# Two PSUM banks per vector and scalar instruction in the feed-forward parts of a hybrid decoder layer (fp32, one core)

## The chip, the cores and the metric

The kernel runs on one core of one Trainium2 chip. The metric is the device time of one execution in microseconds; given are three executions of the kernel before, and one more was recorded by the hardware profiler. Engines are called PE (matrix products), DVE (vector), ACT (scalar), POOL and SP. POOL only builds constants here and SP only starts transfers.

## What is computed

One step of a hybrid decoder layer on 1024 prompt tokens and 8 x 4 sample tokens, 1056 in all, width 1024, in fp32. The parts that the change touches are the two feed-forward parts:

```
def rmsnorm(x, g):
    y = x * rsqrt(mean(x * x) + EPS)
    return y * g

def swiglu_ffn(x, w_gu, w_down):
    gate, up = split(x @ w_gu)          # D_FF = 2816 each
    return (silu(gate) * up) @ w_down

x = x + 0.5 * rmsnorm(swiglu_ffn(rmsnorm(x, g1), w_gu1, w_down1), g2)
x = x + mixer(x)                        # convolution and RG-LRU heads, one projection in, one out
x = x + 0.5 * rmsnorm(swiglu_ffn(rmsnorm(x, g3), w_gu2, w_down2), g4)
x = x + rmsnorm(sigmoid(rmsnorm(x, g5) @ w_gate) * (p @ w_proj), g6)
```

## The kernel before, in words

**Layout.** Features lie on the 128 partitions, tokens along the free axis. The 1056 tokens are three chunks of C = 352 (c = 0, 1, 2). Every fp32 product is three matmuls of a high and a low part (`passes`, lines 589 to 591): x_hi, x_lo, the weights' w_hi, w_lo and wd_hi, wd_lo, and the hidden values' a_hi, a_lo. ACT makes a high part by a copy, DVE the low part by a subtraction. The first norm's gain is folded into the weights, its 1/rms (`rstd_pre`) is multiplied onto the products.

**Steps.** D_FF is worked in NI = 11 steps of G = 2 blocks of 128. A step has, per chunk, four gate and up products of 24 matmuls (into four PSUM banks: g0, g1, u0, u1), and later eight down products of 6 matmuls (m = 0 to 7) that DVE adds into `acc`. In steps 2 to 10 (a hardware loop, `ffn_step`) the order on PE is the gate and up products of chunks 0, 1, 2 and then the down products of chunks 0, 1, 2. In the last step (`ffn_last`) each chunk's down products stand right behind its gate and up products, so that the norm behind the part can begin chunk by chunk. The first step of part 1 follows the tokens as they come in; the first step of part 2 (`ffn_first`) has the down products of chunks 0 and 1 behind chunk 1 and those of chunk 2 behind chunk 2.

**Banks.** Six PSUM banks are a ring, `ps`. `ring_plan` numbers each use n of the whole program, use n lies in bank n mod 6, and PE may write it when `psum_free` has reached n - 5; the reader counts `psum_free` up by one for each bank. Two more banks (`ps_aux`) hold the small products of the norms.

**From products to hidden values.** On DVE `scaled` reads g0, g1, u0, u1 one by one (line 1583); ACT takes the silu of each half (`silu`, line 1089); DVE multiplies each half (`hidden`, line 1594); ACT rounds each half to a_hi (`hidden_hi`, line 1098); DVE makes each half of a_lo (`hidden_lo`, line 1600), upon which PE's `down_products` may begin. `down` (lines 1645 and 1650) reads the down products' banks one by one.

**Order.** It is written out by hand for each engine; each runs its own list in order and waits on counters. In the last step DVE's list for chunk 1 and 2 puts between the eight `down` the four parts of `apply_pair` for the chunk before (lines 1554 to 1568: 1/rms, gain, residual, low part, squares into `ssum`, line 1526); PE waits for the finished sum of squares with its small product of line 628.

```
                    hidden_chunk(f, i, c, tiles(f, i), hook)
                    pair(0)
                    for m in range(KT):
                        down(f, i, c, m)
                        if m in (2, 5, 7):
                            q = 1 + (2, 5, 7).index(m)
                            pair(q)
```

At the start, PE turns the parameter rows and the state rows into one bank (lines 752 to 756), and DVE copies it out in three pieces (lines 1718 to 1720).

Of the kernel before, what the change touches and what calls it, by code (L numbers as in the profile page):

```python
# [62 lines left out]
def ring_plan():  # L63
# [9 lines left out]
    for c in range(NC):  # L73
        for k in range(KT):
            put("xT", c, k)
        if c == 0:
            put("params")
        n += 4
# [109 lines left out]
def cols(c):  # L188
    return slice(C * c, C * c + C)


def build(nc, a, out):
    ctx = ExitStack()
    with ctx:
# [250 lines left out]
        def _(sp_eng):  # L445
# [94 lines left out]
            eng.wait_ge(a_lo_done, 2 * NI * NC * G)  # L540
# [36 lines left out]
        def _(eng):  # L577
# [67 lines left out]
            def down_products(f, i, c):  # L645
                Q, off = NI * NC * G * f, down_at(f, i, c)
                eng.wait_ge(a_lo_done, i * (NC * G) + (Q + 2 * c + 2))
# [97 lines left out]
            for c in range(NC):  # L745
# [3 lines left out]
                if c == 0:  # L749
# [3 lines left out]
                    eng.transpose(dst[:, P:P + CW * NJ], rows[0:CW * NJ, P:2 * P],  # L753
                                  ident[0:CW * NJ, 0:CW * NJ])
# [242 lines left out]
        def _(eng):  # L997
# [84 lines left out]
            def silu(f, i, c, h):  # L1082

                R, Q = RING["ffn", f], NI * NC * G * f
                q, n = NC * G * i + (Q + 2 * c + h), STEP * i + (gate_at(f, i, c) + h)
                eng.wait_ge(psum_free, n + 1)
                if f or not isinstance(i, int) or i or c:
                    eng.wait_ge(prod_done, q - 1)
                eng.activation(tmp_s[:, h, :], tmp_g[:, h, :], ACT.Silu).then_inc(silu_done, 1)  # L1089

            def hidden_hi(f, i, c, h):

                R, Q = RING["ffn", f], NI * NC * G * f
                eng.wait_ge(prod_done, NC * G * i + (Q + 2 * c + h + 1))
# [3 lines left out]
                eng.activation(a_hi[:, h, cols(c)], tmp_a[:, h, :], ACT.Copy).then_inc(a_hi_done, 1)  # L1098

            def hidden_chunk(f, i, c, next_half, hook=None):  # L1100
# [3 lines left out]
                silu(f, i, c, 0)  # L1104
                hook("g0")
                silu(f, i, c, 1)
# [5 lines left out]
                hidden_hi(f, i, c, 0)  # L1112
                hidden_hi(f, i, c, 1)
# [352 lines left out]
        def _(eng):  # L1466
# [16 lines left out]
            def bank_at(reg, n):  # L1483

                eng.wait_ge(psum_full, reg + (n + 1))
                return ps[:, n % BANKS, 0:C]
# [88 lines left out]
            def scaled(f, i, c, h, up):  # L1575

                R, Q = RING["ffn", f], NI * NC * G * f
                q, off = NC * G * i + (Q + 2 * c + h), gate_at(f, i, c) + 2 * up + h
                src = bank_at(i * STEP, off)
                if f or not isinstance(i, int) or i or c:  # L1580

                    eng.wait_ge(prod_done if up else silu_done, q - 1)
                eng.tensor_tensor((tmp_u if up else tmp_g)[:, h, :], src, rstd_pre[:, cols(c)],  # L1583
                                  ALU.mult).then_inc(psum_free, 1)

            def hidden(f, i, c, h):

                R, Q = RING["ffn", f], NI * NC * G * f
                q, n = NC * G * i + (Q + 2 * c + h), STEP * i + (gate_at(f, i, c) + 2 + h)
                eng.wait_ge(silu_done, q + 1)  # L1590
                eng.wait_ge(psum_free, n + 1)
                if f or not isinstance(i, int) or i or c:
                    eng.wait_ge(a_lo_done, q - 1)
                eng.tensor_tensor(tmp_a[:, h, :], tmp_s[:, h, :], tmp_u[:, h, :], ALU.mult  # L1594
                                  ).then_inc(prod_done, 1)

            def hidden_lo(f, i, c, h):
                q = NC * G * i + (NI * NC * G * f + 2 * c + h)
                eng.wait_ge(a_hi_done, q + 1)
                eng.tensor_tensor(a_lo[:, h, cols(c)], tmp_a[:, h, :], f32(a_hi[:, h, cols(c)]),  # L1600
                                  ALU.subtract).then_inc(a_lo_done, 1)

            def hidden_chunk(f, i, c, next_tile, hook=None):
# [5 lines left out]
                scaled(f, i, c, 0, 0)  # L1609
                hook("g0")  # L1610
                scaled(f, i, c, 1, 0)
# [630 lines left out]
```

## Time and profile before

| | |
|---|---|
| device time, three executions | 2345.4, 2345.52, 2349.55 us; median 2345.52 us |
| profiled execution, first to last instruction (span) | 2337.7 us |
| its own device time | not listed apart; the median stands 7.8 us above the span |
| PE busy | 2158.0 us, 92% of the span, 13020 matmuls |
| DVE busy | 1317.6 us, 56%, 2620 instructions |
| ACT busy | 769.8 us, 33%, 1500 instructions |
| mean granted PE clock | 0.959 of full speed |
| moved by DMA | 116.15 MB, mean 50 GB/s |

Busy time overlaps between engines. A busy share tells how full an engine is, not what sets the end; for that one reads who waited for whom, and in which stretch. The loops of the two feed-forward parts lie at about 125 to 745 us and 1427 to 2047 us; the last steps reach to about 860 us and 2160 us.

### The profile page before, as it was taken

To read this page: it belongs to the slowest core of one execution; us is meant where nothing else is said; L and a number is where in the kernel's file an instruction comes from. 1 tells how busy PE (TensorE), PEld (TensorE's weight loads), DVE (VectorE), ACT (ScalarE), POOL (GpSimd) and SP (SyncE) were. 2 spreads that over 40 slices of the span, in tenths; PEclk is the share of its full clock that TensorE was granted. 3 is DMA by queue.
4 is the path that set the end of the run, shared out by engine and by line. 5 is a ranking of instruction groups with operands and counts; after the bars stand their busy time and mean duration, and the time that the engine had idled before them with its cause. 6 is when DMAs were issued, how large, how long until landed. Compare 5 with 4: busy or idle time off the path is not lost. (4 is left out here: it accounts for less than half of the span.)

```text
span 2337.7 us, 34611 instructions
## 1 busy us (share of the span) xinstructions
PE 2158.0 (92%) x13020; PEld 2106.1 (90%) x13020; DVE 1317.6 (56%) x2620; ACT 769.8 (33%) x1500; POOL 0.9 (0%) x8
## 2 busy tenths in 40 slices
PE   5899999999999878999989689999999999995886
PEld 5899999999999878887789689999999999995886
DVE  4544444543445666988555764545434554557686
ACT  4311121221122333365575532212221121225563
POOL 0000000000000000000000000000000000000000
PEclk8999999999999889999999889999999999998897
DMA  4101111101111011100014201111101111102222
GB/s 149 37 28 45 54 54 54 54 27 35 45 54 54 1 45 41 46 1 19 19 38 144 91 1 55 55 54 54 45 18 45 54 54 54 54 1 73 72 91 75
DMA packets 92360, 116.15 MB, mean 50 GB/s; under 512 B 4596, under 2 KB 83704, under 8 KB 92282
## 3 DMA queue, kind: packets, MB, share of 16 engines
q1 hardware_dynamic: 91065, 110.79, 14.4%
q10 hardware_dynamic: 1216, 4.33, 0.6%
q8 instruction: 48, 0.79, 0.1%
q14 instruction: 31, 0.25, 0.0%
HBM read 110.15 MB, written 4.95 MB: 49 GB/s over the span
## 5 line engine op out<-in xcount | busy, mean ns | idle before, releaser
L589 PE MATMUL ps<-x_hi,w_lo 128*128 128x352 f32 x2688 | 883.2, 329 | 17.8 <-DVE w_lo L1503 8.8
L590 PE MATMUL ps<-x_lo,w_hi 128*128 128x352 f32 x2688 | 872.9, 325 | 0.0
L591 PE MATMUL ps<-x_hi,w_hi 128*128 128x352 f32 x2688 | 871.9, 324 | 0.0
L589 PEld LDWEIGHTS ps<-x_hi,w_lo 128*128 128x128 f32 x2688 | 514.6, 191 | 19.1 <-DVE w_lo L1503 9.5
L590 PEld LDWEIGHTS ps<-x_lo,w_hi 128*128 128x128 f32 x2688 | 515.3, 192 | 0.0
L591 PEld LDWEIGHTS ps<-x_hi,w_hi 128*128 128x128 f32 x2688 | 513.5, 191 | 0.0
L589 PE MATMUL ps<-a_hi,wd_lo 128*128 128x352 f32 x1104 | 361.6, 328 | 24.6 <-DVE a_lo L1600 11.6
L590 PE MATMUL ps<-a_lo,wd_hi 128*128 128x352 f32 x1104 | 357.7, 324 | 0.0
L591 PE MATMUL ps<-a_hi,wd_hi 128*128 128x352 f32 x1104 | 357.3, 324 | 0.0
L1650 DVE TENSOR_TENSOR acc<-ps,acc 128x352 f32<-128x352 f32 x480 | 249.3, 523 | 88.7 <-PE ps L591 82.8
L1583 DVE TENSOR_TENSOR tmp_u<-ps,rstd_pre 128x352 f32<-128x352 f32 x132 | 69.1, 524 | 370.7 <-PE ps L591 370.7
L1022 ACT ACTIVATE w_hi<-raw,params 128x256 fp32r<-128x256 f32 x512 | 213.6, 496 | 132.0 <-DMA raw<-in_ffn_w_gu_dram 109.1
L1503 DVE SCALAR_TENSOR_TENSOR w_lo<-raw,params,w_hi 128x256 fp32r<-128x256 f32 x512 | 225.8, 477 | 46.7 <-ACT w_hi L1022 46.7
L1089 ACT ACTIVATE tmp_s<-tmp_g 128x352 f32<-128x352 f32 x132 | 65.3, 498 | 552.1 <-DVE tmp_g L1583 552.1
L589 PEld LDWEIGHTS ps<-a_hi,wd_lo 128*128 128x128 f32 x1104 | 210.4, 191 | 27.6 <-DVE a_lo L1600 12.8
L590 PEld LDWEIGHTS ps<-a_lo,wd_hi 128*128 128x128 f32 x1104 | 210.9, 191 | 0.0
L591 PEld LDWEIGHTS ps<-a_hi,wd_hi 128*128 128x128 f32 x1104 | 210.1, 190 | 0.0
L1583 DVE TENSOR_TENSOR tmp_g<-ps,rstd_pre 128x352 f32<-128x352 f32 x132 | 68.5, 522 | 244.1 <-PE ps L591 230.0
L1098 ACT ACTIVATE a_hi<-tmp_a 128x352 fp32r<-128x352 f32 x132 | 59.9, 494 | 418.4 <-DVE tmp_a L1594 418.4
L829 PE MATMUL ps<-gp,diag 128*128 128x352 f32 (+1 forms) x360 | 108.8, 460 | 3.5 <-ACT diag L1284 3.5
L1526 DVE TENSOR_TENSOR ssum<-ssum,sq 128x352 f32<-128x352 f32 x177 | 92.6, 523 | 22.3 <-ACT sq L1048 9.5
L829 PEld LDWEIGHTS ps<-gp,diag 128*128 128x128 f32 x360 | 69.2, 194 | 38.1 <-issue 5.5
(172 smaller groups left out, 1678.2 us busy)
## 6 DMA issues: line engine op xcount, KB each, us to landing
raw<-in_ffn_w_gu_dram SPq DMA_DIRECT2D x88, 512.0 KB, 3.5
rawd<-in_ffn_w_down_dram SPq DMA_DIRECT2D x22, 1024.0 KB, 7.6
raw<-in_w_out_dram SPq DMA_DIRECT2D x24, 512.0 KB, 3.5
raw<-in_ple_w_gate_dram SPq DMA_DIRECT2D x24, 512.0 KB, 3.4
raw<-in_w_in_dram SPq DMA_DIRECT2D x16, 512.0 KB, 4.0
x_in<-in_x_prompt_dram ACTq DMA_DIRECT2D x6, 512.0 KB, 7.8
out_dram<-y_stage SPq DMA_DIRECT2D x6, 512.0 KB, 2.8
rawd<-in_ple_w_proj_dram SPq DMA_DIRECT2D x1, 1024.0 KB, 7.2
```

The lines of the kernel that those rows point to most:

```text
L589: eng.matmul(dst, wl, xh, start=first, stop=False)
L590: eng.matmul(dst, wh, xl, start=False, stop=False)
L591: return eng.matmul(dst, wh, xh, start=False, stop=last)
L829: mm = eng.matmul(dst[:, 0:w], diag[:, tap, :], gp[:, j, at0:at0 + w], start=tap == 0, stop=tap == TP - 1)
L1022: ins = eng.activation(w_hi[s][:, sl], raw[:, sl], ACT.Copy, scale=vec(gain, k))
L1089: eng.activation(tmp_s[:, h, :], tmp_g[:, h, :], ACT.Silu).then_inc(silu_done, 1)
L1098: eng.activation(a_hi[:, h, cols(c)], tmp_a[:, h, :], ACT.Copy).then_inc(a_hi_done, 1)
L1503: ins = eng.scalar_tensor_tensor(w_lo[s][:, sl], raw[:, sl], vec(gain, k), f32(w_hi[s][:, sl]), ALU.mult, ALU.subtract)
L1526: eng.tensor_tensor(ssum[:, i % 2, :], ssum[:, i % 2, :], sq[:, (ADD0[i] + m - 1) % SQ, :], ALU.add).then_inc(add_done, 1)
L1583: eng.tensor_tensor((tmp_u if up else tmp_g)[:, h, :], src, rstd_pre[:, cols(c)], ALU.mult).then_inc(psum_free, 1)
L1650: eng.tensor_tensor(acc[:, m, cols(c)], src, acc[:, m, cols(c)], ALU.add).then_inc(psum_free, 1)
```

## The change

DVE and ACT take the two banks of a pair in one instruction of 2 x 352 elements: `scaled` reads g0 and g1 together, then u0 and u1 together; `silu`, `hidden`, `hidden_hi` and `hidden_lo` work on both halves at once; `down` reads banks m and m + 1. A reader waits until both banks are full, and counts `psum_free` up by two. Since the pairs have to begin on an even bank, the states at the start get a ring use of their own ("states"). Where `ffn_last` put `apply_pair` behind m = 2, 5, 7 it now stands behind the pairs that begin at m = 2, 4, 6.

```
@@ ring_plan
         if c == 0:
             put("params")
+            put("states")
@@ PE, start
+                    mm.then_inc(psum_full, 1)
+                    dst = bank(RING["states"], 512)
                     for j in range(NJ):
-                        mm = eng.transpose(dst[:, 2 * P + 32 * j:2 * P + 32 * j + 32],
+                        mm = eng.transpose(dst[:, 32 * j:32 * j + 32],
                                            st_rows[0:32, j * P:j * P + P], ident[0:32, 0:32])
@@ ACT
-            def silu(f, i, c, h):
+            def silu(f, i, c):
...
-                eng.activation(tmp_s[:, h, :], tmp_g[:, h, :], ACT.Silu).then_inc(silu_done, 1)
+                eng.activation(tmp_s[:, :, :], tmp_g[:, :, :], ACT.Silu).then_inc(silu_done, 1)
...
-                eng.activation(a_hi[:, h, cols(c)], tmp_a[:, h, :], ACT.Copy).then_inc(a_hi_done, 1)
+                eng.activation(a_hi[:, :, cols(c)], tmp_a[:, :, :], ACT.Copy).then_inc(a_hi_done, 1)
@@ DVE
-            def bank_at(reg, n):
+            def banks_at(reg, n):
+                assert n % 2 == 0 and BANKS % 2 == 0
+                eng.wait_ge(psum_full, reg + (n + 2))
+                return ps[:, n % BANKS:n % BANKS + 2, 0:C]
...
+            def scaled(f, i, c, up):
+                q, off = NC * i + (NI * NC * f + c), gate_at(f, i, c) + G * up
+                src = banks_at(i * STEP, off)
                 if f or not isinstance(i, int) or i or c:
+                    eng.wait_ge(prod_done if up else silu_done, q)
+                eng.tensor_tensor((tmp_u if up else tmp_g)[:, :, :], src,
+                                  rstd_pre[:, cols(c)].unsqueeze(1).broadcast_to([P, G, C]),
+                                  ALU.mult).then_inc(psum_free, G)
+            def hidden(f, i, c):
+                q, n = NC * i + (NI * NC * f + c), STEP * i + (gate_at(f, i, c) + G)
                 eng.wait_ge(silu_done, q + 1)
-                eng.wait_ge(psum_free, n + 1)
+                eng.wait_ge(psum_free, n + G)
...
+                eng.tensor_tensor(a_lo[:, :, cols(c)], tmp_a[:, :, :], f32(a_hi[:, :, cols(c)]),
                                   ALU.subtract).then_inc(a_lo_done, 1)
...
-                src = bank_at(i * STEP, off)
+                src = banks_at(i * STEP, off)
+                dst = acc[:, m:m + 2, cols(c)]
                 if isinstance(i, int) and i == 0:
-                    eng.tensor_copy(acc[:, m, cols(c)], src).then_inc(psum_free, 1)
+                    eng.tensor_copy(dst, src).then_inc(psum_free, 2)
                     return
...
+                eng.tensor_tensor(dst, src, dst, ALU.add).then_inc(psum_free, 2)
@@ DVE, ffn_last
-                    for m in range(KT):
+                    for m in range(0, KT, 2):
                         down(f, i, c, m)
-                        if m in (2, 5, 7):
-                            q = 1 + (2, 5, 7).index(m)
+                        if m:
+                            q = m // 2
                             pair(q)
@@ DVE, start
-                eng.tensor_copy(params[:, width:3 * P], src[:, width:3 * P]).then_inc(psum_free, 1)
+                eng.tensor_copy(params[:, P:P + CW * NJ], src[:, P:P + CW * NJ]).then_inc(psum_free, 1)
+                eng.wait_ge(psum_full, RING["states"] + 1)
+                eng.tensor_copy(params[:, width:3 * P], ps[:, RING["states"] % BANKS, 0:P]
+                                ).then_inc(psum_free, 1)
```

PE's list keeps its products and their order; only what it waits for counts differently. Two places on the other engines show what moved.

DVE, the last step of feed-forward part 1, chunk 1, before: from the read of u0 and u1 (tmp_u) over the hidden values to the first `down` (acc<-ps,acc) and the next part of the norm's application. In brackets are the counters waited for: prod_done the hidden product, silu_done the silu, a_hi_done the high part, psum_full PE, dve_own and psum_free among others DVE's own.

```order
L1583 TENSOR_TENSOR tmp_u<-ps,rstd_pre 128x352 [waits prod_done,psum_full] x2
L1594 TENSOR_TENSOR tmp_a<-tmp_s,tmp_u 128x352 [waits a_lo_done,psum_free,silu_done] x2
L1600 TENSOR_TENSOR a_lo<-tmp_a,a_hi 128x352 [waits a_hi_done] x2
L1554 TENSOR_TENSOR acc<-acc,rstd_post 128x2x352 [waits aux_free]
L1559 SCALAR_TENSOR_TENSOR acc<-acc,half_g,x_hi 128x352 [waits dve_own]
L1559 SCALAR_TENSOR_TENSOR acc<-acc,half_g,x_hi 128x352
L1563 TENSOR_TENSOR acc<-acc,x_lo 128x2x352 [waits dve_own]
L1650 TENSOR_TENSOR acc<-ps,acc 128x352 [waits psum_free,psum_full] x3
L1554 TENSOR_TENSOR acc<-acc,rstd_post 128x2x352 [waits aux_free]
```

And now:

```order
L1583 TENSOR_TENSOR tmp_u<-ps,rstd_pre 128x704 [waits prod_done,psum_full]
L1594 TENSOR_TENSOR tmp_a<-tmp_s,tmp_u 128x704 [waits a_lo_done,psum_free,silu_done]
L1599 TENSOR_TENSOR a_lo<-tmp_a,a_hi 128x2x352 [waits a_hi_done]
L1555 TENSOR_TENSOR acc<-acc,rstd_post 128x2x352 [waits aux_free]
L1560 SCALAR_TENSOR_TENSOR acc<-acc,half_g,x_hi 128x352 [waits dve_own]
L1560 SCALAR_TENSOR_TENSOR acc<-acc,half_g,x_hi 128x352
L1564 TENSOR_TENSOR acc<-acc,x_lo 128x2x352 [waits dve_own]
L1646 TENSOR_TENSOR acc<-ps,acc 128x2x352 [waits psum_free,psum_full] x2
L1555 TENSOR_TENSOR acc<-acc,rstd_post 128x2x352 [waits aux_free]
```

Three pairs of instructions became three single ones, each of which waits for the whole of the one before it; and ahead of the second L1555 stand four banks of down products instead of three.

ACT, the first step of part 1, chunk 2, before: the table and silu of each half, the high part of the down weights (wd_hi, two blocks of 1024), and the high parts of the next step's weights and of the hidden values.

```order
L1089 ACT_TABLE_LOAD [waits prod_done]
L1089 ACTIVATE tmp_s<-tmp_g 128x352 [waits psum_free]
L1033 ACTIVATE wd_hi<-rawd 128x2048 [waits rawd_in]
L1089 ACTIVATE tmp_s<-tmp_g 128x352 [waits prod_done,psum_free]
L1022 ACTIVATE w_hi_51<-raw,params 128x256 [waits raw_in0,psum_full]
L1022 ACTIVATE w_hi_51<-raw,params 128x256 x3
L1098 ACTIVATE a_hi<-tmp_a 128x352 [waits prod_done] x2
```

And now:

```order
L1091 ACT_TABLE_LOAD [waits prod_done]
L1091 ACTIVATE tmp_s<-tmp_g 128x704 [waits psum_free]
L1036 ACTIVATE wd_hi<-rawd 128x2048 [waits rawd_in]
L1025 ACTIVATE w_hi_51<-raw,params 128x256 [waits raw_in0,psum_full]
L1025 ACTIVATE w_hi_51<-raw,params 128x256 x3
L1100 ACTIVATE a_hi<-tmp_a 128x2x352 [waits prod_done]
```

The down weights' high part now stands behind the silu of both halves instead of one.

## Rows read from the trace of the kernel before

**Rows 1.** The page's first part: busy time, share of the span, instructions of each engine.
```profile
PE 2158.0 (92%) x13020; PEld 2106.1 (90%) x13020; DVE 1317.6 (56%) x2620; ACT 769.8 (33%) x1500; POOL 0.9 (0%) x8
```
**Rows 2.** Busy us (x instructions) of PE, PEld, DVE, ACT, POOL; clock; DMA; one loop stretch.
```profile
200.00:269.00 69.00, 69.00 (x436) 69.00 (x435) 32.34 (x65) 14.01 (x29) 0.00 (x0) 1.00 0.14 46
```
**Rows 3.** Who waited for whom, PE: total us, times, longest us; whole span.
```profile
PE ps_aux L628 <- DVE ssum L1526: 71.9, 10, 11.8
PE ps L589 <- DVE a_lo L1600: 11.6, 5, 2.6
...
PE ps L589 <- issue: 6.7, 3, 2.6
...
PE ps L739 <- DVE x_lo L1757: 5.3, 4, 3.0
...
PE ps L589 <- DVE acc L1645: 0.5, 1, 0.5
```
**Rows 4.** Groups by line and shape: busy us, mean ns of one, idle us before.
```profile
L1650 DVE TENSOR_TENSOR acc<-ps,acc 128x352 f32<-128x352 f32 x480 | 249.3, 523 | 88.7 <-PE ps L591 82.8
...
L1098 ACT ACTIVATE a_hi<-tmp_a 128x352 fp32r<-128x352 f32 x132 | 59.9, 494 | 418.4 <-DVE tmp_a L1594 418.4
...
L1563 DVE TENSOR_TENSOR acc<-acc,x_lo 128x704 f32<-128x704 f32 x44 | 39.2, 892 | 1.5
...
L1077 ACT ACTIVATE x_hi<-acc 128x704 fp32r<-128x704 f32 x32 | 25.4, 793 | 115.6 <-DVE acc L1563 115.6
```
**Rows 5.** DVE in order of time, last step of part 1, chunk 1: start, us, instruction, [idle before].
```profile
787.15 0.52 DVE L1583 TENSOR_TENSOR tmp_u<-ps,rstd_pre 128x352 f32<-128x352 f32 x1 [4.02 <-PE ps L591]
787.59 0.95 DVE L1594 TENSOR_TENSOR tmp_a<-tmp_s,tmp_u 128x352 f32<-128x352 f32 x2
788.67 0.96 DVE L1600 TENSOR_TENSOR a_lo<-tmp_a,a_hi 128x352 fp32r<-128x352 f32 x2
789.54 0.89 DVE L1554 TENSOR_TENSOR acc<-acc,rstd_post 128x704 f32<-128x704 f32 x1
...
792.39 1.38 DVE L1650 TENSOR_TENSOR acc<-ps,acc 128x352 f32<-128x352 f32 x3
793.68 0.88 DVE L1554 TENSOR_TENSOR acc<-acc,rstd_post 128x704 f32<-128x704 f32 x1
794.60 1.08 DVE L1559 SCALAR_TENSOR_TENSOR acc<-acc,half_g,x_hi 128x352 f32<-128x352 f32 x2
```
**Rows 6.** PE in order of time, the same step: chunk 1's down products, and the norm's sum.
```profile
789.68 0.43 PE L589 MATMUL ps<-a_hi,wd_lo 128*128 128x352 f32 x1 [2.57 <-DVE a_lo L1600]
...
811.34 1.44 PE L628 MATMUL ps_aux<-ones,ssum 128*128 128x1 f32 x6 [6.12 <-DVE ssum L1526]
```
**Rows 7.** PE after two such waits: busy us (x matmuls), granted clock, DMA.
```profile
761.00:764.00 3.00, 3.00 (x10) 0.50 0.02 5
...
2062.40:2065.40 3.00, 3.00 (x19) 1.00 0.02 5
```
**Rows 8.** Chunk 0 of part 2's last step: PE's first down matmul, DVE's fourth `down`.
```profile
2062.34 0.40 PE L589 MATMUL ps<-a_hi,wd_lo 128*128 128x352 f32 x1 [2.62 <-issue]
...
2066.43 0.53 DVE L1650 TENSOR_TENSOR acc<-ps,acc 128x352 f32<-128x352 f32 x1 [0.43 <-PE ps L591]
```
**Rows 9.** Last step of part 1, chunk 2: u1, ACT's high parts of weights, DVE's low parts.
```profile
824.73 0.52 DVE L1583 TENSOR_TENSOR tmp_u<-ps,rstd_pre 128x352 f32<-128x352 f32 x1 [3.46 <-PE ps L591]
...
826.56 0.89 ACT L1022 ACTIVATE w_hi<-raw,params 128x256 fp32r<-128x256 f32 x2
...
828.28 0.88 DVE L1503 SCALAR_TENSOR_TENSOR w_lo<-raw,params,w_hi 128x256 fp32r<-128x256 f32 x2 [1.07 <-ACT w_hi L1022]
```
**Rows 10.** ACT between chunk 0 and chunk 1 of the start.
```profile
48.46 0.45 ACT L1190 ACTIVATE x_hi<-ps 128x352 fp32r<-128x352 f32 x1
```
**Rows 11.** DVE at the start: the copies of parameters and states.
```profile
20.27 0.27 DVE L1718 COPY params<-ps 128x104 f32<-128x104 f32 x1 [1.21 <-PE ps L756]
...
20.64 0.28 DVE L1720 COPY params<-ps 128x128 f32<-128x128 f32 x1
```

More of the change, by code:

```diff
@@ L645, in down_products @@
             def down_products(f, i, c):
-                Q, off = NI * NC * G * f, down_at(f, i, c)
-                eng.wait_ge(a_lo_done, i * (NC * G) + (Q + 2 * c + 2))
+                Q, off = NI * NC * f, down_at(f, i, c)
+                eng.wait_ge(a_lo_done, i * NC + (Q + c + 1))
                 for m in range(KT):
@@ L1590, in hidden, with hidden_lo @@
                 eng.wait_ge(silu_done, q + 1)
-                eng.wait_ge(psum_free, n + 1)
+                eng.wait_ge(psum_free, n + G)
                 if f or not isinstance(i, int) or i or c:
-                    eng.wait_ge(a_lo_done, q - 1)
-                eng.tensor_tensor(tmp_a[:, h, :], tmp_s[:, h, :], tmp_u[:, h, :], ALU.mult
+                    eng.wait_ge(a_lo_done, q)
+                eng.tensor_tensor(tmp_a[:, :, :], tmp_s[:, :, :], tmp_u[:, :, :], ALU.mult
                                   ).then_inc(prod_done, 1)
[L1597 to L1600, printed above, removed]
+            def hidden_lo(f, i, c):
+                eng.wait_ge(a_hi_done, NC * i + (NI * NC * f + c + 1))
+                eng.tensor_tensor(a_lo[:, :, cols(c)], tmp_a[:, :, :], f32(a_hi[:, :, cols(c)]),
@@ L1618, in hidden_chunk @@
                         next_tile(0, k)
-                scaled(f, i, c, 1, 1)
-                hidden(f, i, c, 0)
-                hidden(f, i, c, 1)
+                scaled(f, i, c, 1)
+                hidden(f, i, c)
                 if c == 2 and not last:
                     return
-                hidden_lo(f, i, c, 0)
-                hidden_lo(f, i, c, 1)
+                hidden_lo(f, i, c)
                 if c == 2:
@@ L1692, in ffn_last @@
                     pair(0)
-                    for m in range(KT):
+                    for m in range(0, KT, 2):
                         down(f, i, c, m)
-                        if m in (2, 5, 7):
-                            q = 1 + (2, 5, 7).index(m)
+                        if m:
+                            q = m // 2
                             pair(q)
@@ L2135, in _ @@
                     for d in range(2):
-                        for m in range(KT):
+                        for m in range(0, KT, 2):
                             down(1, 0, d, m)
-                            if d == 0 and m in (2, 5):
-                                out_pair(2, 2 + m // 5)
+                            if d == 0 and m in (2, 4):
+                                out_pair(2, 1 + m // 2)
                         if d == 0:
                             invert("pre3", 2)
-            for m in range(KT):
+            for m in range(0, KT, 2):
                 down(1, 0, 2, m)
                 tiles(1, 0)(1, m)
+                tiles(1, 0)(1, m + 1)
             with eng.Fori(1, NI - 1) as i:
```

51 lines of the change are left out of this document (16 added, 35 removed).

## The prediction

> **What bounds the kernel now.** I read the page's shares first: PE is busy 92% of the span, DVE 56%, ACT 33% [rows 1]. So either PE sets the end, or something that PE waits for. The table by stretches separates the two. In the loops of both feed-forward parts, some 1240 us of the span, PE is busy 69.00 of 69.00 us at granted clock 1.00, while DVE is busy 32.3 and ACT 14.0 us [rows 2]. The reader should see that there is nothing to win there: DVE and ACT only have to keep up. Next, the list of PE's waits [rows 3]. By stretch, none of these waits begins in a loop. They lie in the start, in the last step of each part, in the first step of part 2, and in the parts that don't change. Two kinds bear on this change. PE waits for the hidden values' low part (11.6 us in five waits; of those called "issue", 6.7 us in three, two are the same wait at chunk 0 of a last step, 2.6 us each). And PE's small product of line 628 waits for the sum of squares, 71.9 us, up to 11.8 us at a time. In both, DVE's list is what PE waits for, so last I read that list in order of time.
>
> **The head of each chain.** In the last steps, and in chunk 2 of part 2's first step, no product stands between the last up product and the down products, so PE sits idle over a serial chain. In part 1's last step it reads: u1 from 787.15, the two products from 787.59, the low parts from 788.67, PE from 789.68 [rows 5, 6], which is 2.53 us. Halves overlap there: ACT rounds half 0 while DVE multiplies half 1. After the change, four instructions of 704 elements follow each other, each waiting for the whole of the last. The trace has no 704-element instruction on two PSUM banks. The nearest rows are DVE's on 704 elements of SBUF, 892 ns, against 523 ns for 352 out of PSUM, and ACT's copy of 704, 793 ns, against 494 for 352 [rows 4]. From one such DVE instruction to one that waits for it are 0.92 us (793.68 to 794.60) [rows 5]. With 0.03 to 0.06 us for each hand-over the head is 0.92 (u) + 0.91 (product) + 0.83 (ACT) + 0.94 (low part to PE) = 3.60 us: **+1.05 us**. Bounds for the two-bank instruction: 2 x 523 = 1.05 us above; below, 0.81 us, the distance from one 704-element instruction to the next that doesn't wait. I take 0.89, as SBUF and PSUM sources differ little at 352.
>
> **What the pairs save.** Three `down` in a row take 792.39 to 793.68, 0.43 us each; an instruction of 704 is followed by the next after 0.81 us, so a pair saves 0.06 us, and 0.2 us over eight banks. Busy time falls more, 528 pairs x (2 x 0.52 - 0.89), about 83 us of DVE, but that is overlapped write-out, which nobody waits for. The Trainium skill (Perfetto Trace Analysis, Optimizing Scalar/DVE Operations) puts the overhead of a DVE instruction on PSUM at about 125 ns; by that the 19 pairs that stand in chains PE waits for would save 2.4 us instead of 1.1. The sum keeps 0.06.
>
> **Sum, place by place.**
> - Loops: 0. Where DVE waits for PE its `down` stand 0.96 us apart (0.53 of work, 0.43 idle) [rows 8], so a pair of banks takes PE 1.9 us; DVE's pair plus two low parts of weights (0.88 us for two [rows 9], less overlap) is some 1.65 us. The cover is that difference and six banks; it would be gone at 1.1 us per pair. The later release of a bank doesn't reach PE: a pair is free 0.9 us after its second bank is full, while PE comes back to it four banks later.
> - Last step, part 1. Chunk 0: +1.05. Chunk 1: PE's next wait is for the sum of squares (6.12 us, ends 811.34) [rows 6], and DVE works nearly without a pause from 787.15 to there, so the shift of DVE's list counts: +1.05 for the head, -0.2 for the pairs, and a new wait. The second application now stands behind four `down` instead of three. The fourth bank is readable 4.09 us after PE begins [rows 8], i.e. 3.60 + 4.09 = 7.69 us after the start of u; DVE gets there at 3.47 + 2.85 (first application, 789.54 to 792.39) + 0.81 = 7.13. Wait: +0.6. Together +1.45. Chunk 2: DVE waits next for ACT's high parts of weights, begun 1.83 us after the chain's start (824.73 to 826.56) and used by DVE from 828.28 [rows 9]. ACT will get there at 0.92 + 0.91 + 0.72 (its copy of 704, less the overlap with its next instruction) = 2.55: +0.7, less 0.2: +0.5. The step: **+3.0**.
> - Last step, part 2: the same, plus 0.25 where ACT's silu of both halves comes later and PE already waits for the inverse: **+3.25**.
> - First step, part 2: chunk 0's +1.05 passes through DVE's list to the sum of squares, where PE waits anyway, less three pairs: +0.9. Chunk 2: +1.05, less the 0.5 us wait for DVE's copy [rows 3], since banks 0 and 1 are now both read before DVE's low parts of the other weights: +0.6. **+1.5**.
> - Start: between chunks ACT must end a_hi before it can take the next tokens, from 48.46 on [rows 10], and PE waits for the low part made from that (5.3 us in four waits) [rows 3]: +0.7 twice. The down weights' high part stands behind a silu of 0.79 instead of 0.50: +0.3. Against that, two of the three copies at 20.27 to 20.64 [rows 11] no longer wait for the states: -0.4. **+1.4** with rounding.
>
> These make +9.2 us against the profiled execution's 2337.7 us.
>
> **The clock.** After two of the seven waits for a low part PE ran at 0.50 of its clock, 10 matmuls in 3 us instead of 19, i.e. at 1.2 instead of 2.4 GHz; after the other five it stayed at 1.00 [rows 7] (the two rows are chunk 0 of either last step). It followed a 2.62 us wait and spared another as long. Longer waits should make it commoner. One spell costs 9 matmuls x 0.158 = 1.4 us in 3 us, some 1.5 us with its edges. Places where a new spell would count: chunk 0 of part 2, and chunk 1 of both last steps, where it delays the fourth bank for which DVE now waits. Elsewhere a spell is there already or PE waits afterwards anyway. I count two of these three: **+3.0**. Bounds 0 and +4.5.
>
> Total 9.2 + 3.0 = **+12.2 us**: span 2349.9. The median of the runs stands 7.8 us above the profiled span; I add the same difference to it: 2345.5 + 12.2 = **2357.7 us**.
>
> **Rivals.**
> 1. *Same mechanism, no new slow spells*: +9.2, 2354.7 us. For it: five of seven waits left the clock alone. Chance 0.2, beside 0.6 for the forecast.
> 2. *The two-bank instruction is dear.* If it costs what two reads cost (1.05 us), heads grow by 0.16, and the pairs lose 0.1 instead of saving 0.06: about +4 more, with three spells +4.5: 9.2 + 4.0 + 4.5 = 17.7, 2363.2 us. Above 1.1 us the loops also begin to wait. Against it: the products on SBUF take 0.95 us for two and the `down` out of PSUM 1.38 for three [rows 5], the same 0.43 apart, so PSUM as a source adds nothing that doubling could multiply. Chance 0.1.
> 3. *The other side: fewer instructions win.* Place: DVE's lists between 787 and 811 us and their likes, where DVE is nearly full. If a saved instruction gave back its whole 0.16 us of busy time there (19 pairs: 3.0 us), and the head, also rid of four instructions, grew by nothing, the time would be 3.0 + 0.4 less: 2342.1 us. It decides if a 704-element link in the chain is below about 0.63 us (2.53 / 4); the rows of 0.88 to 0.92 for it speak against. The same page of the Trainium skill says that grouping helps a saturated engine and that breaking instructions up helps where an engine isn't saturated but leaves bubbles on another; DVE is the first by its busy share in that stretch and the second by the head of the chain. I follow the head. Chance 0.06.
> 4. *It doesn't do what it says*: an instruction over two banks is taken apart and handed on half by half, the head stays at 2.53 us, and the time at 2345.5 us. The order of instructions shows single ones whose one counter update comes at the end, so 0.04.
>
> **The numbers.** A measurement of this kernel can tell about 0.2%, 4.7 us, from no change. Cases 1, 2 and the forecast (0.9) all lie above 2350.2. Rival 3 ends within 0.2% at its own price; a little beyond is possible. So faster 0.03, within 0.07, slower 0.90. The range takes in the forecast with no spell and a lower head (+5, two-bank link 0.81) and rival 2 with a little for slow spells elsewhere that fall differently: 2350.5 to 2366.
>
> **What would show it.** DVE 2620 - 528 = 2092 instructions, about 1235 us busy; ACT 1368, about 750 us. Two-bank reads near 890 ns. Loops again at 69.00 of 69.00. PE's waits at chunks 0 and 1 of the last steps near 3.65 us instead of 2.6, more rows with clock 0.50 behind them, and the waits for the sum of squares ending 1.5 and 0.5 us later against the chain's start. It is wrong if two-bank reads take over 1.1 us, if PE idles inside the loops, if the head stays near 2.5 us, or if the clock's spells move by more than three anywhere.

## The result, and the profile after

The changed kernel takes **2356.67 us** (median of eight executions, 2353.5 to 2362.41), the kernel before 2343.72 us (eight, 2335.91 to 2349.55): ratio 1.0058, 95% interval 1.0042 to 1.0074. That is 12.95 us more; the forecast was 12.2 more, 2357.7 us, and the range held it.

The page of the changed kernel, its first line and its first part:

```profile
span 2360.4 us, 33167 instructions
...
PE 2168.7 (92%) x13020; PEld 2115.6 (90%) x13020; DVE 1268.8 (54%) x2092; ACT 748.1 (32%) x1368; POOL 0.9 (0%) x8
```

DVE has the 2092 instructions forecast and ACT the 1368; ACT's busy time is as forecast (about 750), DVE's is 34 us higher (1268.8, not 1235). The profiled executions differ by 22.7 us of span (2337.7 and 2360.4), more than the medians. One reason is luck of the clock in code that the change doesn't touch. The same 462 matmuls of the mixer, the first row before, the second after (us, PE busy (x matmuls), granted clock, DMA, GB/s):

```profile
1070.00:1166.00 96.00, 91.58 (x462) 0.98 0.04 13
```
```profile
1078.00:1174.00 96.00, 95.11 (x462) 0.95 0.02 5
```

So single profiles are compared below place by place, and totals by the medians alone.

The loops, as in [rows 2] (the columns there):

```profile
200.00:269.00 69.00, 69.00 (x436) 69.00 (x435) 30.01 (x41) 13.07 (x23) 0.00 (x0) 1.00 0.14 46
```

PE is busy 69.00 of 69.00 us with the same 436 matmuls; DVE gets by with 41 instructions instead of 65. Nothing is won or lost there.

The groups that answer to [rows 4], by line and shape (busy us, mean ns of one, idle before):

```profile
L1646 DVE TENSOR_TENSOR acc<-ps,acc 128x704 f32<-128x704 f32 x240 | 213.7, 891 | 122.8 <-PE ps L592 120.5
L1594 DVE TENSOR_TENSOR tmp_a<-tmp_s,tmp_u 128x704 f32<-128x704 f32 x66 | 58.9, 893 | 6.0
L1583 DVE TENSOR_TENSOR tmp_u<-ps,rstd_pre 128x704 f32<-128x704 f32 x66 | 58.9, 892 | 322.9 <-PE ps L592 276.0 <-issue 46.9
L1100 ACT ACTIVATE a_hi<-tmp_a 128x704 fp32r<-128x704 f32 x66 | 52.3, 793 | 436.3 <-DVE tmp_a L1594 436.3
```

A read of two PSUM banks takes 891 ns, as forecast, and one of two SBUF halves 893. The waits of PE, as in [rows 3]:

```profile
PE ps_aux L629 <- DVE ssum L1527: 74.2, 10, 11.5
PE ps L590 <- DVE a_lo L1599: 17.6, 5, 3.8
PE ps_aux L641 <- DVE std L1542: 13.7, 9, 5.6
...
PE ps L590 <- issue: 9.1, 3, 3.8
```

Five waits for a_lo cost 17.6 us instead of 11.6, 3.8 at most instead of 2.6: +1.20 each. The two among "issue" grew alike (6.7 to 9.1). Waits for the inverse (std) went from 10.3 us in seven to 13.7 in nine; the new ones are of about 1 us. DVE in chunk 1 of part 1's last step, as in [rows 5], and PE and ACT beside it:

```profile
789.62 0.89 DVE L1583 TENSOR_TENSOR tmp_u<-ps,rstd_pre 128x704 f32<-128x704 f32 x1 [5.53 <-PE ps L592]
790.61 0.89 DVE L1594 TENSOR_TENSOR tmp_a<-tmp_s,tmp_u 128x704 f32<-128x704 f32 x1
792.35 0.89 DVE L1599 TENSOR_TENSOR a_lo<-tmp_a,a_hi 128x704 fp32r<-128x704 f32 x1 [0.86 <-ACT a_hi L1100]
793.16 0.88 DVE L1555 TENSOR_TENSOR acc<-acc,rstd_post 128x704 f32<-128x704 f32 x1
...
797.28 0.89 DVE L1646 TENSOR_TENSOR acc<-ps,acc 128x704 f32<-128x704 f32 x1 [1.19 <-PE ps L592]
799.85 0.89 DVE L1646 TENSOR_TENSOR acc<-ps,acc 128x704 f32<-128x704 f32 x1 [1.68 <-PE ps L592]
800.66 0.88 DVE L1555 TENSOR_TENSOR acc<-acc,rstd_post 128x704 f32<-128x704 f32 x1
```
```profile
791.53 0.79 ACT L1100 ACTIVATE a_hi<-tmp_a 128x704 fp32r<-128x704 f32 x1 [5.40 <-DVE tmp_a L1594]
```
```profile
793.30 0.66 PE L590 MATMUL ps<-a_hi,wd_lo 128*128 128x352 f32 x1 [3.77 <-DVE a_lo L1599]
...
817.76 1.44 PE L629 MATMUL ps_aux<-ones,ssum 128*128 128x1 f32 x6 [6.55 <-DVE ssum L1527]
```

The head is now 0.99 (u) + 0.92 (product) + 0.82 (ACT) + 0.95 (low part to PE) = 3.68 us, four instructions strictly behind each other. Then DVE stands idle for 1.19 and 1.68 us ahead of its first two pairs of banks, where three single `down` followed without a gap before [rows 5]. From u to the norm's sum are 28.14 us; before, 24.19 [rows 5, 6].

PE in the 3 us behind each of the seven heads (us, PE busy (x matmuls), granted clock, DMA, GB/s). Five of the waits are of 3.8 us; at chunk 2 of the last steps (third and last row) they are of 3.1 us, where they were 1.9 before:

```profile
763.45:766.45 3.00, 3.00 (x13) 0.65 0.02 5
793.35:796.35 3.00, 3.00 (x10) 0.50 0.00 0
834.82:837.82 3.00, 3.00 (x14) 0.70 0.00 0
1431.69:1434.69 3.00, 3.00 (x10) 0.50 0.00 0
2078.89:2081.89 3.00, 3.00 (x10) 0.50 0.02 5
2108.77:2111.77 3.00, 3.00 (x12) 0.57 0.00 0
2149.44:2152.44 3.00, 3.00 (x12) 0.62 0.00 0
```

All seven now have a stretch at 1.2 GHz; before, two had one [rows 7]. The profile explains a longer chain, a wait of DVE and a slower clock, but not which part of the change brings them, nor what each is worth.

### The profile page after: what moved, and what is told of

Same layout as the page of the kernel before. It is cut to its first block and busy times, and to the rows that moved or that the text cites. A ratio compares the mean times of both kernels' runs of the same rounds, so it can differ in the third digit from the quotient of the medians.

```text
span 2360.4 us, 33167 instructions
## 1 busy us (share of the span) xinstructions
PE 2168.7 (92%) x13020; PEld 2115.6 (90%) x13020; DVE 1268.8 (54%) x2092; ACT 748.1 (32%) x1368; POOL 0.9 (0%) x8
## 5 line engine op out<-in xcount | busy, mean ns | idle before, releaser
L590 PE MATMUL ps<-a_hi,wd_lo 128*128 128x352 f32 x1104 | 365.3, 331 | 29.7 <-DVE a_lo L1599 17.6
L1646 DVE TENSOR_TENSOR acc<-ps,acc 128x704 f32<-128x704 f32 x240 | 213.7, 891 | 122.8 <-PE ps L592 120.5
L1504 DVE SCALAR_TENSOR_TENSOR w_lo<-raw,params,w_hi 128x256 fp32r<-128x256 f32 x512 | 216.6, 478 | 89.3 <-ACT w_hi L1025 89.3
L1583 DVE TENSOR_TENSOR tmp_u<-ps,rstd_pre 128x704 f32<-128x704 f32 x66 | 58.9, 892 | 322.9 <-PE ps L592 276.0
L1091 ACT ACTIVATE tmp_s<-tmp_g 128x704 f32<-128x704 f32 x66 | 52.3, 793 | 561.3 <-DVE tmp_g L1583 561.2
L1100 ACT ACTIVATE a_hi<-tmp_a 128x704 fp32r<-128x704 f32 x66 | 52.3, 793 | 436.3 <-DVE tmp_a L1594 436.3
L1583 DVE TENSOR_TENSOR tmp_g<-ps,rstd_pre 128x704 f32<-128x704 f32 x66 | 58.8, 891 | 239.4 <-PE ps L592 225.5
L1527 DVE TENSOR_TENSOR ssum<-ssum,sq 128x352 f32<-128x352 f32 x177 | 92.6, 523 | 22.7 <-ACT sq L1051 10.3
```

What stands on the lines that cost most here:

```text
L590: eng.matmul(dst, wl, xh, start=first, stop=False)
L1091: eng.activation(tmp_s[:, :, :], tmp_g[:, :, :], ACT.Silu).then_inc(silu_done, 1)
L1100: eng.activation(a_hi[:, :, cols(c)], tmp_a[:, :, :], ACT.Copy).then_inc(a_hi_done, 1)
L1504: ins = eng.scalar_tensor_tensor(w_lo[s][:, sl], raw[:, sl], vec(gain, k), f32(w_hi[s][:, sl]), ALU.mult, ALU.subtract)
L1527: eng.tensor_tensor(ssum[:, i % 2, :], ssum[:, i % 2, :], sq[:, (ADD0[i] + m - 1) % SQ, :], ALU.add).then_inc(add_done, 1)
L1583: eng.tensor_tensor((tmp_u if up else tmp_g)[:, :, :], src, rstd_pre[:, cols(c)].unsqueeze(1).broadcast_to([P, G, C]), ALU.mult).then_inc( ...
```

## The experiments

Ten kernels in twelve runs follow (e12 is e6 again, e13 is e11 again), each beside the kernel before on the same chip. The theory: the loss comes from the hidden values' chain taken in pairs where PE waits for its end (the seven heads), and the clock multiplies it; the pairs of down banks and the loops cost nothing. Rivals: the down pairs, with their wait for a fourth bank and their late release, or the PSUM reads of two banks themselves, carry it.

### e1: only the down banks in pairs

```
-                eng.tensor_tensor((tmp_u if up else tmp_g)[:, :, :], src, ...
-                                  ALU.mult).then_inc(psum_free, G)
+                eng.tensor_tensor(dst[:, h, :], src, rstd_pre[:, cols(c)], ALU.mult
+                                  ).then_inc(psum_free, 1)
...
```
(the same by halves, two instructions each, for silu, hidden, hidden_hi, hidden_lo, in every chunk of every step)

> Down products read in pairs, hidden values made by halves as before. If the longer head (u, product, high part, low part as single 704-element instructions) is the cause, all seven waits of PE for the low part are back at 2.57 us (1.9 at chunk 2 of a last step), against 3.77 in the changed kernel; few of them are followed by a slow spell of the clock; the time is that of before within 0.2% (0 to +2 us, for the second application of the norm standing behind four down products). If the pairs of down products were the cause, the time would stay at that of the change, some +13 us.

Measured: 2343.57 us beside 2342.09, ratio 1.0008 (0.9995 to 1.0022). PE's waits for a_lo:

```profile
PE ps L601 <- DVE a_lo L1630: 11.6, 5, 2.6
```

They are those of the kernel before, and the loss is gone but for what can't be told from nothing. The down pairs by themselves, 264 fewer instructions on DVE, show neither a cost nor a gain, with an interval from a gain of 1 us to a cost of 5.

One cost of theirs is seen in the profile all the same. In chunk 2 of a last step PE waits for a bank of down products to come free, 1.59 and 1.62 us before. Two banks released together come free later: 2.00 and 1.95 us in e1, and each time the clock falls behind the wait (0.56), where it had stayed at 1.00. The first of the two, and the 3 us behind it:

```profile
830.54 0.43 PE L601 MATMUL ps<-a_hi,wd_lo 128*128 128x352 f32 x1 [2.00 <-DVE acc L1687]
```
```profile
830.59:833.59 3.00, 3.00 (x11) 0.56 0.08 28
```

The sum of the prediction has no term for it. In the changed kernel the wait doesn't appear; there the head ahead of it is 1.2 us longer.

### e2 and e3: the chain in pairs everywhere, and only away from the heads

e2 has the chain in pairs and the down banks one by one. e3 is the changed kernel with halves in the last steps and in chunk 2 of part 2's first step, chosen by

```
+def halves_apart(f, i, c):
+    return isinstance(i, int) and (i == NI - 1 or (f, i, c) == (1, 0, 2))
...
+                sl, k = (slice(0, 2), 2) if h is None else (h, 1)
+                eng.activation(a_hi[:, sl, cols(c)], tmp_a[:, sl, :], ACT.Copy).then_inc(a_hi_done, k)
```

The second line of the diff is one of the writing, not of the question: to let pairs and halves share a counter, a pair raised it by two.

> Hidden values as single 704-element instructions, down products bank by bank and the norm's parts behind banks 2, 5, 7 as before. Head theory: seven waits at 3.77 us, slow spells behind most of them, +8 to +13 us against before; DVE's wait ahead of the second application in chunk 1 shorter than in the change, since it stands behind three banks again. Rival (down pairs): time of before.

> The changed kernel with halves again only where PE waits for the head: the last step of each part and chunk 2 of part 2's first step; loops and start stay in pairs. Head theory: like the one with down pairs only, plus 1.4 us for the start, so +1 to +3 us against before; loops 69.00 of 69.00 busy. If anything in the loops cost time, it would lie above that by what the loops cost.

Measured: e2 2368.92 us, ratio 1.0116 (1.0097 to 1.0136), 12 us slower than the changed kernel with less of the change in it. e3 2351.47 us, 1.0038 (1.0025 to 1.0052), with the waits at the heads back at 2.6 us as expected, and yet some 9 us over before. Both missed. No theory of pairs explains that e2 is slower than the changed kernel, so I looked for a difference of the writing. At the start of e3 ACT's table load for the silu waited for the gate products that DVE scales (tmp_g); in the changed kernel it doesn't. That made the step of two the suspect, and e7, e8 and e9 settle it.

### e7: the chain in pairs, counters in steps of one, down banks one by one

```
-                src = banks_at(i * STEP, off)
-                dst = acc[:, m:m + 2, cols(c)]
+                src = bank_at(i * STEP, off)
+                dst = acc[:, m, cols(c)]
...
-                eng.tensor_tensor(dst, src, dst, ALU.add).then_inc(psum_free, 2)
+                eng.tensor_tensor(dst, src, dst, ALU.add).then_inc(psum_free, 1)
```

> The hidden chain in pairs everywhere exactly as in the changed kernel (each instruction raises its semaphore by one), the sums of the down products bank by bank in the order of the kernel before. Theory (the longer head of the chain carries the loss, the pairs of the down banks next to nothing): TensorE's waits for a_lo stay at 17.6 us for 5, the time stays within 1.5 us of the changed kernel, ratio to before 1.0045 to 1.006. Rival (the wait for the fourth bank and the late release in pairs carry a good part of it): 1.002 or less. The earlier run of this edit (e2_hidden_only) raised the semaphores by two and is not counted on here: if its 1.0116 was that of the pairs themselves, this one shows it too.

Measured: 2358.04 us beside 2344.01, ratio 1.0059 (1.0044 to 1.0073), the whole of the change's loss without its down pairs. Its waits for a_lo, and DVE between its low part and the second application in chunk 1:

```profile
PE ps L590 <- DVE a_lo L1604: 17.6, 5, 3.8
```
```profile
796.90 0.52 DVE L1651 TENSOR_TENSOR acc<-ps,acc 128x352 f32<-128x352 f32 x1
798.11 0.53 DVE L1651 TENSOR_TENSOR acc<-ps,acc 128x352 f32<-128x352 f32 x1 [0.70 <-PE ps L592]
799.70 0.52 DVE L1651 TENSOR_TENSOR acc<-ps,acc 128x352 f32<-128x352 f32 x1 [1.07 <-PE ps L592]
```

The application no longer stands behind a fourth bank, and DVE still waits, 1.77 us, for banks two and three; its application begins at 800.15, 6.91 us after a_lo (793.24), against 8.31 in the changed kernel (792.35 to 800.66). So the pair adds 1.4 us at this place in this profile, but the total doesn't show it: with e1 on the other side, the chain carries the loss and the down pairs none that can be measured.

### e8: e3 again, counters in steps of one

```
-                sl, k = (slice(0, 2), 2) if h is None else (h, 1)
+                sl, k = slice(0, 2) if h is None else h, 1
```
(each wait asks for the number of instructions, not of halves)

> As e3_tail_halves (halves in the last steps and in chunk 2 of the second part's first step, pairs elsewhere), but every instruction of the chain raises its semaphore by one, whatever it covers. Theory (in e3 the step of two held the silu's table load behind the product with the gate and lengthened each hand-over): the start costs 1.2 us as in the changed kernel, the first step of part 2 about 1, the heads nothing, so 2.5 us over before, ratio 1.0005 to 1.0015. Rival (the pairs of the start and the first step are as dear as e3 showed, whatever the semaphores do): 1.0035 or more, as e3.

Measured: 2344.14 us beside 2344.01, ratio 1.0005 (0.9993 to 1.0016). PE's waits:

```profile
PE ps L626 <- DVE a_lo L1654: 11.6, 5, 2.6
...
PE ps L776 <- DVE x_lo L1821: 6.5, 4, 3.8
```

The heads carry the loss: 59 of the 66 chunks keep the pairs of the chain (all but the seven at the heads), every down bank is in pairs, and what is left is 0.1 us by the medians, with an interval to 3.7 us (e11 and e13 below come back to it). The start still pays, 6.5 us in four waits for the tokens' low part instead of 5.3 [rows 3].

### e9: the changed kernel with steps of two, nothing else

```
-                eng.activation(tmp_s[:, :, :], tmp_g[:, :, :], ACT.Silu).then_inc(silu_done, 1)
+                eng.activation(tmp_s[:, :, :], tmp_g[:, :, :], ACT.Silu).then_inc(silu_done, 2)
```
(likewise prod_done, a_hi_done, a_lo_done, with every wait for twice the number)

> The changed kernel with one difference: silu_done, prod_done, a_hi_done and a_lo_done count halves, so that each paired instruction raises its semaphore by two (and each wait asks for twice the number). Theory: the waits of the silus move ahead of their table loads (1.06 us of it in the open at the start) and each hand-over in the head takes longer, heads of 4.4 us instead of 3.8, so 10 us over the changed kernel, ratio to before 1.010 to 1.012. Rival (a step of two costs nothing, e2 and e3 were slow for the mixture of forms): 1.0058 as the changed kernel.

Measured: 2371.55 us beside 2344.01, ratio 1.011 (1.0092 to 1.0129). A counter raised by two instead of one costs as much again as the change. The load of the silu's table is one place where it shows. ACT in chunk 2 of the start, first the changed kernel, then e9:

```profile
94.96 0.46 ACT L1068 ACTIVATE rstd_pre<-ps_aux 128x352 f32<-128x352 f32 x1 [4.30 <-PE ps_aux L641]
95.44 1.28 ACT L1091 ACT_TABLE_LOAD   x1
96.74 0.79 ACT L1091 ACTIVATE tmp_s<-tmp_g 128x704 f32<-128x704 f32 x1
```
```profile
93.48 0.46 ACT L1079 ACTIVATE rstd_pre<-ps_aux 128x352 f32<-128x352 f32 x1 [4.30 <-PE ps_aux L652]
95.00 1.28 ACT L1103 ACT_TABLE_LOAD   x1 [1.05 <-DVE tmp_g L1607]
96.29 0.79 ACT L1103 ACTIVATE tmp_s<-tmp_g 128x704 f32<-128x704 f32 x1
```

With steps of one the load runs while DVE works, and only the silu has to wait for DVE; with steps of two the load itself waits. Here 1.05 us come into the open, and PE's wait for the down weights' low part behind it is 3.96 us instead of 2.94. Over all eight such loads ACT's wait ahead of them goes from 0.1 to 21.2 us, first the changed kernel, then e9:

```profile
L1091 ACT ACT_TABLE_LOAD x8 | 10.3, 1283 | 0.1
```
```profile
L1103 ACT ACT_TABLE_LOAD x8 | 10.3, 1283 | 21.2 <-DVE tmp_g L1607 18.0 <-issue 3.2
```

Second, the head: DVE in chunk 1 of part 1's last step, with PE's wait after it:

```profile
791.28 0.89 DVE L1607 TENSOR_TENSOR tmp_u<-ps,rstd_pre 128x704 f32<-128x704 f32 x1 [5.47 <-PE ps L603]
792.38 0.89 DVE L1622 TENSOR_TENSOR tmp_a<-tmp_s,tmp_u 128x704 f32<-128x704 f32 x1 [0.20 <-DVE tmp_u L1607]
794.24 0.89 DVE L1630 TENSOR_TENSOR a_lo<-tmp_a,a_hi 128x704 fp32r<-128x704 f32 x1 [0.97 <-ACT a_hi L1113]
```
```profile
795.19 0.66 PE L601 MATMUL ps<-a_hi,wd_lo 128*128 128x352 f32 x1 [4.00 <-DVE a_lo L1630]
```

u to product is 1.10 us (0.99 before the step of two), product to low part 1.86 (1.74): PE waits 4.00 us instead of 3.77. (The "4.4" of the expectation was a distance from matmul to matmul, where 3.8 was a wait; on the scale of the wait it should have read 4.0.) Why the hand-over itself takes longer no view shows. Nor do the two add up to the whole: seven heads at 0.23 us and 1.05 us at the start are 2.7 of some 12 us. In the last steps PE's longest waits for the inverse also grow, from 0.9 and 1.1 us to 2.3 and 2.5; how the rest comes about stays open.

### e5, e6, e12: what the clock's spells are worth

Unused matmuls of 160 columns go ahead of the seven heads, their results unread: 40, 40 and 32 of them at chunks 0, 1 and 2 of the last steps and 40 at chunk 2 of part 2's first step in the changed kernel (e5), 26, 26, 18 and 26 in the kernel before (e6, and e12 once more). They leave nothing of the computation out.

```
+            def filler(c, n, count):
+                eng.wait_ge(aux_free, n)
+                for k in range(count):
+                    eng.matmul(ps_aux[:, (n - 1) % 2, C:512], x_hi[:, k % KT, C * c:C * c + P],
+                               x_hi[:, k % KT, C * c:C * c + 512 - C], start=True, stop=True)
...
+                    head_filler(f, post, c)
                     down_products(f, i, c)
```

> The changed kernel, with 32 to 40 small matmuls (stationary 128 columns, moving 160) on PE ahead of each of the seven waits for the low part, into free columns of a norm's bank; their results are used by nobody. The chain on DVE and ACT is as in the change, so if only its length counts, the time stays at +13 us. If the slow spells of the clock behind these waits are a cost of their own, PE stays at 1.00 behind all seven and the time falls by the spells that count, 1.5 us each at up to five places: -5 to -8 us against the change, +5 to +8 against before.

> The kernel before with 26, 26, 18 and 26 unused matmuls of 160 columns ahead of the heads of the down products (last steps' chunks 0 to 2, first step of part 2), as e5 had in the changed kernel. Theory (a slow spell of the clock behind a wait is a cost of its own, and two of seven heads had one): waits at the heads stay 2.6 us or grow by 0.2, the two spells go, 2 to 3 us faster than before, ratio 0.9985 to 0.9995. Rival (spells that go at the heads come back elsewhere, or the unused matmuls delay the heads as much): 1.000 or more.

> The same kernel as e6_before_filled, beside e13 on one chip. If the unused matmuls are worth in the kernel before what e6 showed, the ratio to before is 0.9965 to 0.998 again; if e6 was luck of its executions, 0.999 or more.

Measured: e5 2350.13 us, ratio 1.0027 (1.0016 to 1.0038) instead of the change's 1.0058; e6 2338.35 us, **0.9972** (0.9962 to 0.9982); e12 2338.51 us, **0.998** (0.9969 to 0.9991). Behind the fillers the clock stays up. Two of e5's seven stretches behind the heads, in place of 0.65 and 0.50 above:

```profile
764.29:767.29 3.00, 3.00 (x21) 1.00 0.00 0
793.09:796.09 3.00, 3.00 (x21) 1.00 0.02 5
```

And DVE's two pairs of down banks in chunk 1 of e5:

```profile
795.27 0.89 DVE L1664 TENSOR_TENSOR acc<-ps,acc 128x704 f32<-128x704 f32 x1
797.21 0.89 DVE L1664 TENSOR_TENSOR acc<-ps,acc 128x704 f32<-128x704 f32 x1 [1.04 <-PE ps L593]
```

The wait is 1.04 us instead of 2.87. Some 0.5 us of it is the fillers' doing, which were too many: PE starts 1.44 us after the low part begins (791.60 to 793.04) instead of 0.95. So without a spell the wait would be some 0.6 us, an estimate, and the spell made up the rest.

The fillers win 0.31% in the changed kernel and 0.20 to 0.28% in the kernel before. The difference between the two gains, 0.03 to 0.11%, is smaller than the intervals. So the medians don't show that the change makes the spells dearer.

The profiles say more. PE's products and their order are the same in all these kernels, so their profiles can be compared by counting matmuls (without the fillers). Taken together are matmuls 4500 to 6000, 7500 to 8000 and 11500 to the end: the last steps, part 2's first step and what follows each.

| | no fillers | fillers |
|---|---|---|
| halves at the heads | 721.7 (before), 724.2 (e1), 722.9 (e8) us | 717.7 (e6), 719.3 (e12), 720.9 (e10), 720.8 (e11), 719.6 (e13) us |
| pairs at the heads | 737.9 (the change), 735.7 (e7) us | 729.6 us (e5) |

By the means the pairs cost 13.9 us without fillers and 9.9 us with them: some 10 us are the chain's length (and what e5's fillers themselves delay), and some 4 us go with the clock. These are estimates from few profiles, which differ by up to 3 us among themselves. The fillers win 3.3 us where the heads are halves, and 7.2 us where they are pairs. Against the 3.3 stand 5.4 to 5.7 us in the medians of e6 and e12; where the rest is, single profiles can't say. Part of the gain is seen behind the last step of part 1, where nothing was edited: PE's wait for ACT's diagonals in the mixer, before and e6, is

```profile
PE ps L829 <- ACT diag L1284: 3.5, 1, 3.5
```
```profile
PE ps L847 <- ACT diag L1302: 2.2, 1, 2.2
```

It is 3.3 to 5.1 us in the eight profiles without fillers and 1.8 to 2.4 us in the six with them.

### e10, e11, e13: fillers with parts of the change

e10 is e1 with e6's fillers, e11 and e13 are e8 with them.

> e8_tail_unit (pairs in the loops, halves in the last steps and in chunk 2 of the second part's first step) with the unused matmuls of e6 ahead of the seven heads. If e8's start and first step are all that is left of the change's loss, about 1 us over e6: 2337 to 2340 beside a before of 2343.5, ratio 0.9975 to 0.9985. If the pairs kept have a cost that the clock's spells hid in e8, 0.999 or more.

> e1_down_only (the hidden chain by halves everywhere, the down banks summed in pairs) with the unused matmuls of e6 ahead of the seven heads. The pairs of the down banks were free in e1, so the same as e6: ratio 0.997 to 0.998; a value of 0.999 or more would say that pairing the down banks costs something once the spells are gone.

> The same kernel as e11_tail_filled, on the chip of e12. If the pairs it keeps cost something beside the filled kernel before, it stands 0.1 to 0.4% above e12 again, at 0.9995 to 1.0015; if e11 was luck, within 0.1% of e12.

Measured: e10 2337.78 us, 0.9989 (0.9976 to 1.0002); e11 2342.56 us, 1.0009 (0.9998 to 1.002); e13 2343.11 us beside e12's 2338.51 on the same chip, 0.9995 (0.9986 to 1.0005). e11 missed its 0.9975 to 0.9985, and e13 stands 0.15 to 0.2% over e12 again: with the fillers in, the pairs kept in the start, the loops and part 2's first step cost some 4 us, where e8 showed nothing. The fillers kept the clock up at the heads there too (e11's seven stretches all read 1.00). What the pairs cost at the start is in the waits (1.2 us for the tokens' low part). The down pairs don't carry the rest: e10 has them too and stands 4.8 us below e11 on the same chip, at the level of e6 and e12 (2337.78 beside 2338.35 and 2338.51 us). The loops don't either: from matmul 600 to 4500 all fourteen profiles take 619.79 us, within 0.01. Where the rest lies stays open. In the profiles of e11 and e13 it is mostly in the mixer (matmuls 6000 to 7500), 306.0 and 305.7 us against 300.2 in e10, but there e6 has 305.4 as well.

By its ratio e10 (0.9989) falls between its two readings, since the kernel before was faster beside it (2341.34 us); its interval overlaps e6's. The fastest here are the kernel before with fillers, and that with the down pairs added; these runs can't tell the two apart.

## Why the prediction was right, and where it wasn't

**What bounds it, loops at 0.** Right. PE's figures in [rows 2] and in the row after agree to the digit, and part 1's loop takes 619.79 us in every profile, with pairs or without.

**The head, +1.05.** Mechanism right, size 1.20. The row of 892 ns was a good stand-in (891). Short were the hand-overs: u to product is 0.99 us, not 0.92, and the wait holds 0.09 us beside the 3.68 of the chain (3.77 in all) where it held 0.04 before (2.57 and 2.53). e1 and e8 against e7 show that this chain at seven places is the loss, but for what their intervals leave.

**A pair saves 0.06 us.** Not contradicted, and too small to see: e1's interval (from 0.9995) leaves at most 0.05%, 1.2 us, of gain. The estimate of 2.4 us by the Trainium skill's 125 ns (Perfetto Trace Analysis, Optimizing Scalar/DVE Operations) lies outside that, unless the later release of the banks takes it back; e1 measures both together. The other rule of that page of the Trainium skill, that breaking instructions up helps where an engine isn't saturated but leaves bubbles on another, is what e8 does at the heads, and the runs agree: 11.6 us of waits instead of 17.6, 12 us of time.

**Last steps, +3.0 and +3.25, with 0.6 for the fourth bank.** The order of events was right, the wait too where the clock stays up (e5). With a spell behind the head it is 2.87 us, and from u to the norm's sum are 3.95 us more, not 1.45. e7 shows that most of such a wait (1.77 us) comes without the down pairs: the sum booked it under the wrong part. The wait for a bank in chunk 2, longer by 0.4 us in e1, was missing from the sum.

**First step of part 2 (+1.5) and start (+1.4).** The start's term is seen in the waits for the tokens' low part, 6.5 instead of 5.3 us: right in kind, and e8's total doesn't contradict it. PE's 600th matmul starts at 130.2 to 133.7 us in the five profiles with halves at the start and at 133.0 to 135.7 in the six with pairs and steps of one, 2.6 us later by the means. That the wait for the inverse (std) would show new entries of about 1 us wasn't forecast.

**The clock, +3.0 for two new spells that count.** Direction right, the count too small: five new ones in this profile, one at each head that had none (e7, with the same chain, has three). I took from [rows 7] that a 2.62 us wait sometimes brings a spell; at 3.8 it was every time. Their cost, some 4 us by the count of matmuls, is near the 3.0; since two were priced and more came, that is partly luck. The ratios alone, 7.3 us between the change and e5 and 4.7 to 6.6 between before and e12 or e6, don't tell this term from nothing.

**The total** is right within 0.8 us. By the count of matmuls the last steps and the first step cost at most some 10 us without the spells, where the sum had 3.0, 3.25 and 1.5, together 7.75; this part and the clock's both seem to have been set a little low. With the start's 1.2 us these estimates come to some 15 us, more than the 12.95 of the medians; profiles are too few to close that gap. What supports the forecast is the place (heads), the sign and the rough split, not the digits.

**From span to median.** I called 7.8 us the difference between the profiled span and the median. The device time of the changed kernel's profiled execution is 2.0 us above its span (2362.41 and 2360.4); if it is so before, the other 5.8 were that the profile came from a fast execution in a spread of 14 us. Adding the difference to the median was harmless; comparing the two profiles' spans would have shown 22.7 us for a change of 13.

**DVE's 1235 us busy** was wrong by 34. I took all 528 pairs at 2 x 0.52 - 0.89 = 0.15. The halves of products and low parts followed each other already, so joining them saves 0.06 each (tmp_a: 62.7 us for 132 before, 58.9 for 66 now). By groups DVE lost 67 us, and in the total, where the overlapping ends of neighbours count once, 48.8.

**Rivals.** No new spells: refuted by the seven stretches. A dear two-bank read: refuted, 891 ns. Fewer instructions win: refuted by e1 and e7. Taken apart by the hardware: refuted by x240 single instructions of 704.

## What to carry to other kernels

Pairing instructions costs nothing where the engine waits for its producer or where another engine's queue covers it, and costs at the end of a chain for which the busiest engine waits, here 1.2 us for a chain of four links; so pair in the loop and keep halves at the heads (e8), and don't expect a gain from a lighter engine that wasn't the bound. When a producer and consumer are rewritten with a common counter, look in the trace at what waits, and keep steps of one, or the experiment measures its own bookkeeping (e2, e3, e9). And a wait of the matmul engine can cost more than its length, since its clock may come back at half; cheap unused matmuls in it won 0.2 to 0.3% (e5, e6, e12), though only part of that is traced to the heads.

## What was not expected of the hardware

- Raising a counter by two instead of one at four places of the chain cost 0.52% (1.011 against 1.0058): the silu's 1.28 us table load waits for DVE too (21.2 us over eight loads instead of 0.1), and each head takes 0.23 us longer (4.00 against 3.77).
- How often the clock fell behind a head goes with the length of the wait. In the eight profiles without fillers: behind none of eight waits of 1.9 us, 7 of 20 of 2.6 us, 6 of 8 of 3.1 to 3.4 us, and all 20 of 3.8 to 4.4 us; where it fell, PE took 10 to 14 matmuls in 3 us instead of 19. Length is not all of it: behind the 2.0 us waits for a bank in e1, e3 and e8, which come some 8 us after a head, it fell six times of six. After fillers it stayed at 1.00 behind all seven heads, with 20 or 21 matmuls.
- Executions of one kernel differ by up to 15 us by themselves, some of it by the granted clock in places that no edit touched (0.98 and 0.95 for the same 462 matmuls).
